# Two transformer blocks in one kernel: the output projections' last slabs tile by tile, GpSimd's norm factors in another order, and a weight ring that starts at another buffer

## The reference, cut to what matters

```python
# block 1
h = rms_norm(x, mix_pre_norm);  proj = h @ w_in          # 1024 x 2472, then conv, delta rule, attention
mixed = concatenate([o_gdn, o_mla]) @ w_out
x = x + rms_norm(mixed, mix_post_norm)
h = rms_norm(x, ffn_pre_norm)
f = square(relu(h @ w_up)) @ w_down
x = x + rms_norm(f, ffn_post_norm)
# block 2
mod = c @ w_ada + b_ada;  sh1, sc1, gt1, sh2, sc2, gt2 = split(mod)
h = modulate(rms_norm(x, g_pre_mix), sh1, sc1);  proj = h @ w_in_2
mix_out = (sigmoid(ga) * y_conv + sigmoid(gb) * y_attn) @ w_out_2
x = x + gt1 * rms_norm(mix_out, g_post_mix)
h2 = modulate(rms_norm(x, g_pre_mlp), sh2, sc2)
x = x + gt2 * rms_norm(square(relu(h2 @ w_mlp_in)) @ w_mlp_out, g_post_mlp)
```

## Time and profile before

| | |
|---|---|
| median of 3 runs | 3013.69 us (3012.06 to 3013.9) |
| profiled execution | 3016.73 us, span 3014.9 us |
| TensorE busy | 2878.8 us, 95% of the span |
| VectorE, GpSimd, ScalarE busy | 1600.4, 1022.5, 738.2 us |
| TensorE's mean granted clock | 0.983 of 2.4 GHz |

### The profile page before, as it was taken

The page is one execution under the profiler, slowest core; times in us unless marked ns, Lnnn a source line. Parts: engine busy times, 40 slices in busy tenths (PEclk is TensorE's granted clock), DMA queues, the critical chain, the costliest instruction groups (busy, mean ns, idle before and its releaser), DMA issues.

```text
span 3014.9 us, 42598 instructions
## 1 busy us (share of the span) xinstructions
PE 2878.8 (95%) x16394; PEld 2323.0 (77%) x16394; DVE 1600.4 (53%) x1957; ACT 738.2 (24%) x1485; POOL 1022.5 (34%) x706
## 2 busy tenths in 40 slices
PE   7999998979999999999899999989998999999998
PEld 6887567868788888888688886657877888888886
DVE  3455544662777777777832004773246445445546
ACT  3223654323301111111410004562124101110111
POOL 3321001438433333433433321212376332323332
PEclk9999999989999999999999999999999999999999
DMA  3210000023222223222311110001132111111111
GB/s 125 56 28 16 10 1 23 3 86 104 70 84 85 84 82 90 77 83 84 105 49 49 55 29 28 22 1 56 56 133 64 42 54 43 56 42 45 52 49 63
DMA packets 213439, 172.18 MB, mean 57 GB/s; under 512 B 15543, under 2 KB 188878, under 8 KB 213326
## 3 DMA queue, kind: packets, MB, share of 16 engines
q1 hardware_dynamic: 160670, 135.47, 14.6%
q10 hardware_dynamic: 52656, 35.13, 3.9%
HBM read 162.19 MB, written 8.39 MB: 57 GB/s over the span
## 4 chain that ended last, share of the span: by engine, by line
PE 86%; DVE 6%; ACT 3%; POOL 3%; issue 2%; DMA 1%; SPq 0%; ACTq 0%; POOLq 0%; DVEq 0%
PE ps L910 13%; PE ps L912 13%; PE ps L911 13%; PE ps L1338 8%; PE ps L1339 7%; PE ps L1340 7%; PE ps L1130 2%; PE ps L1036 2%; PE ps L929 1%; PE ps L931 1%; PE ps L930 1%; PE ps L1058 1%; PE ps L1534 1%; PE ps L1276 1%; PE ps L1277 1%
## 5 line engine op out<-in xcount | busy, mean ns | idle before, releaser
L295 POOL TENSOR_SCALAR slab_hi<-raw 128x1024 fp32r<-128x1024 f32 (+1 forms) x236 | 268.0, 1136 | 1513.8 <-PE ps L912 576.8
L910 PE MATMUL ps<-act_hi,slab_hi 128*128 128x512 f32 x1472 | 577.0, 392 | 9.0 <-POOL slab_lo L298 7.2
L298 POOL TENSOR_TENSOR slab_lo<-raw,slab_hi 128x1024 fp32r<-128x1024 f32 (+1 forms) x236 | 578.7, 2452 | 19.7
L912 PE MATMUL ps<-act_hi,slab_lo 128*128 128x512 f32 x1472 | 574.6, 390 | 0.0
L911 PE MATMUL ps<-act_lo,slab_hi 128*128 128x512 f32 x1472 | 574.3, 390 | 0.0
L2530 DVE TENSOR_TENSOR acc<-ps,acc 128x512 f32<-128x512 f32 x512 | 339.0, 687 | 197.4 <-PE ps L1340 197.1
L1338 PE MATMUL ps<-slab_hi,hid_hi 128*128 128x512 f32 x1024 | 403.5, 394 | 1.4 <-DVE acc L2530 1.4
L1339 PE MATMUL ps<-slab_hi,hid_lo 128*128 128x512 f32 x1024 | 399.3, 390 | 0.0
L1340 PE MATMUL ps<-slab_lo,hid_hi 128*128 128x512 f32 x1024 | 399.2, 390 | 0.0
L910 PEld LDWEIGHTS ps<-act_hi,slab_hi 128*128 128x128 f32 x1472 | 277.6, 189 | 66.7 <-POOL slab_lo L298 7.5
L1924 ACT ACTIVATE relu<-ps 128x512 f32<-128x512 f32 x128 | 77.1, 602 | 1025.6 <-PE ps L912 1013.7
(11 more groups left out here) (315 smaller groups left out, 4190.0 us busy)
## 6 DMA issues: line engine op xcount, KB each, us to landing
raw<-in_w_in SPq DMA_DIRECT2D x56, 512.0 KB, 3.8
w_ada<-in_w_ada ACTq DMA_DIRECT2D x48, 512.0 KB, 4.1
raw<-in_w_out SPq DMA_DIRECT2D x32, 512.0 KB, 3.6
raw<-in_w_up SPq DMA_DIRECT2D x32, 512.0 KB, 4.0
raw<-in_w_down SPq DMA_DIRECT2D x32, 512.0 KB, 3.5
raw<-in_w_mlp_in SPq DMA_DIRECT2D x32, 512.0 KB, 4.0
raw<-in_w_mlp_out SPq DMA_DIRECT2D x32, 512.0 KB, 3.5
x_tok<-in_x SPq DMA_DIRECT2D x8, 512.0 KB, 6.1
```

The source lines that it names most:

```text
L295: pool.tensor_scalar(self.hi[s][:, 0:width], self.raw[r][:, 0:width], 1.0, 0.0, ALU.mult, ALU.add)\
L298: pool.tensor_tensor(self.lo[s][:, 0:width], self.raw[r][:, 0:width], self.hi[s][:, 0:width].bitcast(F32), ALU.subtract).then_inc(self.spl ...
L910: pe.matmul(o, hi[:, w], a_hi[:, k, cols], start=(k == 0), stop=False)
L912: mm = pe.matmul(o, lo[:, w], a_hi[:, k, cols], start=False, stop=(k == nk - 1))
```

## The change

It has four parts. R2 starts at the buffer that R1 frees first (2, then 0, 1), and its two start waits are gone; four small buffers change places with it. In the output projections the last three slabs are done tile by tile, all of them behind `ready(15)`; the turns of EARLY follow tile 0 and tile 2 in place of slabs 13 and 14. GpSimd does split 12 ahead of the EARLY post factors and places pre factors between the splits of 14 and 15 and behind 15; the LATE factors come one by one, with the FFN's slab 1 among them and slabs 2 and 3 behind them. ScalarE and VectorE follow with single tiles. At the end of the first FFN R5's slab 0 is split behind factor ffn_post 6, slab 1 behind n3 5, instead of both behind ffn_post 7.

```diff
-        R2 = Ring(sem, GDN_PANELS, raws[:3], slab_hi[:3], slab_lo[:3], R1)
+        turned_on = (2, 0, 1)
+        R2 = Ring(sem, GDN_PANELS, [raws[r] for r in turned_on], [slab_hi[r] for r in turned_on],
+                  [slab_lo[r] for r in turned_on], R1, (*turned_on, 3))
...
-            R2.start(sp)
...
-            R2.start_split(pool)
...
+        LATE_NORMS = ((0, 4), (0, 5), (1, 4), (0, 6), (1, 5), (0, 7), (1, 6), (1, 7))
...
-                for m in range(first, 12):
+                for m in range(first, 13):
                     ring.split(pool, 0, m // ring.nraw, m)
                 norm_rstd(post, EARLY)
-                norm_rstd(pre, EARLY)
-                for m in range(12, 16):
+                for m, ts in ((13, ()), (14, (0, 1)), (15, (2, 3))):
                     ring.split(pool, 0, m // ring.nraw, m)
+                    norm_rstd(pre, ts)
                 ffn_splits(following, 0, range(1))
-                for j in range(2):
-                    ffn_splits(following, 0, range(1 + j, 2 + j))
-                norm_rstd(post, LATE)
-                norm_rstd(pre, LATE)
-                ffn_splits(following, 0, range(3, 4))
+                for n, t in LATE_NORMS:
+                    norm_rstd((post, pre)[n], [t])
+                    if (n, t) == (0, NT - 2):
+                        ffn_splits(following, 0, range(1, 2))
+                ffn_splits(following, 0, range(2, 4))
...
-                if (tag, t) == ("ffn_post", NT - 1):
-                    for j in range(2):
-                        R5.split(pool, 0, 0, j)
+                if (tag, t) == ("ffn_post", NT - 2):
+                    R5.split(pool, 0, 0, 0)
+                elif (tag, t) == ("n3", 5):
+                    R5.split(pool, 0, 0, 1)
...
-                for m in range(16):
+                for m in range(13):
...
-                    if m in (13, 14):
+                ring.ready(pe, 0, 15)
+                for t in range(4):
+                    for m in range(13, 16):
+                        mm = out_tile(ring, m, t, a_hi, a_lo)
...
+                    if t == 0:
                         pe.wait_ge(sem("mixed_done"), 16 * run + 12)
-                        turn(pre, acc, 0, scaled(pre, 0), ks=range(4 * (m - 13), 4 * (m - 13) + 4))
+                    if t in (0, 2):
+                        turn(pre, acc, 0, scaled(pre, 0), ks=range(2 * t, 2 * t + 4))
...
-                    if first:
-                        turn_done(pre, 0)
-                    up(i, 0)
+                    up(i, 0, as_split(pre, 0) if first else None)
...
+                late(0)
+                norm_full(pre, 0, act_hi, scale, bias, ks=range(4))
+                late(1)
+                late_square(4)
+                late(2)
+                norm_scale(pre, 4)
+                norm_full(pre, 0, act_hi, scale, bias, ks=range(4, KD))
+                late_square(5)
+                late(3)
+                norm_scale(pre, 5)
+                for t in (6, 7):
+                    late_square(t)
+                    norm_scale(pre, t)
                 norm_full(pre, 1, act_hi, scale, bias)
...
+                post_norm(post, row, EARLY, ready)
+                post_norm(post, row, (4,), ready)
+                norm_split(pre, 0, act_hi, act_lo, gain, ks=range(4))
+                post_norm(post, row, (5,), ready)
+                norm_split(pre, 0, act_hi, act_lo, gain, ks=range(4, KD))
+                post_norm(post, row, (6, 7), ready)
+                norm_split(pre, 1, act_hi, act_lo, gain)
```

More of the change, by code:

```diff
@@ L250, with __init__ @@
     SLOTS = 4
-    def __init__(self, sem, total, raws, his, los, after=None):
+    def __init__(self, sem, total, raws, his, los, after=None, order=range(SLOTS)):
         self.raw, self.hi, self.lo = raws, his, los
         self.nraw, self.nslab, self.total = len(raws), len(his), total
-        self.raw_full = [sem(f"w_raw_full{r}") for r in range(self.SLOTS)]
+        self.raw_full = [sem(f"w_raw_full{r}") for r in order]
         self.carrier = sem("wait_carrier")
@@ L401, in two_blocks @@
         probs = [sb(f"probs{i}", kb, [P, SEQ]) for i, kb in enumerate((9, 13, 17, 25))]
[L402 to L405, removed]
+        probs_t = [sb(f"probs_t{i}", kb, [P, HALF]) for i, kb in enumerate((37, 39, 199.25, 201.25))]
+        wq_nope = sb("wq_nope", 41, [P, 2, P])
+        wq_rope = sb("wq_rope", 42, [P, 2, P])
+        wk = sb("wk_pair", 43, [P, P])
         w_kv = sb("w_kv_all", 45, [P, 1024])
-        sm_max, sm_neg, sm_sum, sm_rec = [sb(n, 40 + 0.0625 * x, [P, 2, NT])
+        sm_max, sm_neg, sm_sum, sm_rec = [sb(n, 44 + 0.0625 * x, [P, 2, NT])
                                           for x, n in enumerate(("sm_max", "sm_neg", "sm_sum", "sm_rec"))]
@@ L1895, in out_projection, with late @@
                     take(1, 0, t)
-                norm_full(pre, 0, act_hi, scale, bias)
-                for t in range(4):
+                def late(t):
                     take(1, 1, t)
@@ L2488, in _, with post_norms @@
             dve.wait_ge(sem("post_gain_in"), 16)
-            for h, tiles in enumerate((EARLY, LATE)):
-                post_norm("mix_post", mix_post_row, tiles, lambda t: dve.wait_ge(sem(f"x_in{t}"), 32))
-                norm_split("n2", h, act_hi, act_lo, ffn_pre_gain)
+            def post_norms(post, pre, row, ready, gain=None):
+                post_norm(post, row, EARLY, ready)
[5 more added lines that the diff above has]
+                norm_split(pre, 1, act_hi, act_lo, gain)
+            post_norms("mix_post", "n2", mix_post_row, lambda t: dve.wait_ge(sem(f"x_in{t}"), 32), ffn_pre_gain)
             def modulation(i, j):
@@ L2721, in _ @@
             dve.wait_ge(sem("gate_rows_done"), 2)
-            for h, tiles in enumerate((EARLY, LATE)):
-                post_norm("mix_post2", gate_rows[0], tiles, lambda t: dve.wait_ge(sem(f"x_in{t}"), 48))
-                norm_split("n4", h, act_hi, act_lo)
+            post_norms("mix_post2", "n4", gate_rows[0], lambda t: dve.wait_ge(sem(f"x_in{t}"), 48))
             ffn_sums(R11, 1, "ffn_post2", gate_rows[1])
```

20 lines of the change are left out of this document (14 added, 6 removed).

## The result

The changed kernel takes **3019.36 us** (median of 20 runs, 3015.64 to 3026.77), the kernel before 3013.99 us (20 runs, 3009.67 to 3017.6). The ratio is 1.002 with a 95% interval of 1.0014 to 1.0027, so the change costs 4.2 to 8.1 us; the medians differ by 5.4. The forecast was 3016.0 us, range 3004 to 3024. The profiled execution of the changed kernel took 3025.83 us (span 3024.0), near the top of its own runs, so the 9.1 us by which its span is longer than that of before overstates the change.

What follows compares the result with a forecast made beforehand. TensorE was taken as the bound, its chain ending last for 86% of the span. Terms 0 + 1.8 + 1.6 - 1.1 = +2.3 us on 3013.7 gave 3016.0 us, range 3004 to 3024.

Steps and rivals of the forecast that it cites:

- A: Whole kernel: the forecast itself, waits change place; 3016.0 us, own range 3008 to 3020, chance 0.46.
- B: Projections: split 15 done in time, ready(15) waits at most 1.5 us; about 3005 us, chance 0.25.
- C: Projections: late 4 us wait stays; 3022 to 3026 us, chance 0.29; decides if first projection's last scale is later than 774.
- The opening, 0 forecast: Opening: panel 0 starts near 111.9, TensorE then waits for conv_tanh until 142.6; net 0, bounds -3.3 and +0.5.
- So the 3.9 us move from L910 to L965. I take 0: Opening: the wait ahead of panel 0 reappears behind panel 1, for panel 0's conv_tanh; net 0.
- First projection, +1.8 forecast: First output projection: 4.5 us wait at ready(15), 1.6 for the clock, late wait 1.5 instead of 4.06; net +1.8 us.
- the 1.6 forecast: First output projection: 1.6 us lost to the lowered clock behind the wait at ready(15).
- The lower bound: First output projection: without any turns in splits 13 and 14 (3.1 of the 4.5 us) it gains 1.0.
- Second projection, +1.6 forecast: Second output projection: +4.5 and +1.6 at ready(15), early waits of 5.9 us go; net +1.6 us, bounds -6 and +5.
- 3.4 us of turns: Second projection's late transposes: splits of slabs 2 and 3 run beside VectorE's first pairs, 3.4 us more of turns.
- R5, -1.1 forecast: First FFN to second block: earlier split of slab 0, TensorE starts at about 1495.1; -1.1 us, bounds -4 and +1.
- ScalarE's copies hidden: First output projection: the four copies that mixed_done asks for end at 741.4, hidden in the slow first tiles.

Runs made afterwards that it cites:

- E1: Kernel before with the opening's part alone (buffer order 2, 0, 1, start waits gone, four small buffers moved): 3018.49 us, +4.5, ratio 1.0013.
- E11: Kernel before with opening's part plus a wait for conv_silu_done, R5's moved splits, and two-slab tile-by-tile projections: 3007.74 us, -6.3, ratio 0.9976.
- E3: Kernel before with R5's two splits moved ahead in the FFN's end, alone: 3010.69 us, -3.3, ratio 0.9986.
- E8: Kernel before with both projections' part, two slabs tile by tile instead of three, GpSimd's factors placed differently: 3013.21 us, -0.3, ratio 1.0.
- E2: Kernel before with the part on both output projections alone: 3019.14 us, +5.1, ratio 1.0018.
- E7: Kernel before with both projections' part, but GpSimd keeps its old order (eight early factors, then splits 12 to 15): 3022.9 us, +9.4, ratio 1.0038.
- E9: E2 with the one wait for split 15 taken apart into three in tile 0, one ahead of each slab's products: 3020.81 us, +6.8, ratio 1.0023.
- E6: Kernel before with ring order 2, 0, 1 and moved small buffers, but both start waits kept: 3012.77 us, -0.8, ratio 1.0001.
- E4: Changed kernel with VectorE's post-norm of the fourth tile cut to 8 of 1024 columns in both projections: 3016.49 us, ratio to before 1.0002.
- E12: Changed kernel with the second ring's fourth and fifth split behind conv_silu_done, and split 15's wait taken apart into three: 3015.95 us, +1.9, ratio 1.0008.
- E5: E1 with GpSimd's fourth and fifth split of the second ring held behind conv_silu_done: 3011.78 us, -1.8 against before, ratio 0.9993.

## Why the prediction was right, and where its terms were off

The forecast (A, waits change place) is what happened: +5.4 us against +2.3, no wait of a part vanished without another in its place. B is out, since both waits for slab 15 are 4.5 us. C's point of decision, a last scale behind 774, was not reached: the late turn starts at 773.33, in a trace that is 2.0 us late already at slab 4, and the late wait shrank to 1.33 and 1.98 us.

The mechanism is right; that the sum came out as near as it did is in part luck. Run alone, the parts measured +4.5, +5.1 and -3.3 us where 0, +3.4 and -1.1 were forecast: R5's part, 2.2 us better than its term, hides half of what the opening's term missed.

**The opening, 0 forecast, the mis-sized step.** All instants stand: start at 112.00 (111.9 forecast), splits over the gate chain and over the product, wait until 143.01 (142.6). The term that was mis-sized is the sum behind it, "So the 3.9 us move from L910 to L965. I take 0". The waits grew by 2.2 us (3.86 + 1.94 before, 0.89 + 7.12 now), and the clock gave back only 1.5: behind the two waits before, 1.6 and 3.3 us were lost to it, behind the one wait now 3.4. That is the 0.7 us of the table, 48.2 against 47.5. Besides, I read the baseline from one trace, and in three of the six with the old ring order the second wait is 0.3 to 0.5 us and the clock takes 1.7 behind it. Against the mean of the six the new opening is 1.8 us (changed kernel) and 2.0 (E1) longer up to panel 2.

Another 2 us or so are lost before the first projection (484.6 to 486.6 us, mean 486.2, in the eight with the new ring order, 484.1 in the mean of the six with the old), where no instruction was changed. It is mostly a count of clock falls between 200 and 330 us. Seven of the eight have two, between 231 and 239 and between 309 and 318, and E11 the second alone (484.6). Of the six, before and E3 have two (near 237 and 250), E8 two (235 and 313), E2, E7 and E9 none (482.4 to 482.7). The fall of 309 to 318 us stands, where it occurs, within 1.1 us behind a wait of 1.93 us that all fourteen traces have; why the clock falls there in one kernel and not in another was not found. Neither the early start (E6 has the fall without it) nor anything else was shown to be its cause. This stays open, and so does how much of E1's +4.5 it is.

**First projection, +1.8 forecast.** Up to the second half of the FFN's panels the term was right: from slab 4 to them it took 93.5 us in the changed kernel and 92.3 in E2, 90.7 to 92.4 in six kernels with the old projection (mean 91.3), so 1.0 to 2.2 more. The wait was 4.52 (4.5), no wait at slab 12, the late wait 1.33 (1.5). The clock cost more than the 1.6 forecast: tile 0 took 7.05 us in the changed kernel, 6.0 in E2, for 18 products that take 4.2 at full speed (a panel's 48 take 11.19). The lower bound took 3.1 of the 4.5 us for turns in splits 13 and 14 (which makes a gain of 1.3, not 1.0); E4, with the fourth tile cut, took off 1.85. What I missed comes behind it: VectorE's second set of sums for the modulation in the FFN's first step starts 5.2 us later than before (786.52 against 781.32), GpSimd's next splits only 4.7 later (787.34 against 782.67), so three of the four sums take turns with a split instead of two, and TensorE waits 3.53 us at 792.78 (3.30 in E2) where it waited 2.27 at 786.85 before. By the end of the FFN, projection 0 costs 2.1 (E2) to 4.6 us.

**Second projection, +1.6 forecast**, measured +2.4 and +2.6. The waits are where they were put: 4.52 at slab 15, none in the early turn, 1.72 (2.1 forecast) ahead of the panels, 2.08 + 2.58 in the late transposes, where 3.4 us of turns were computed. The late wait stayed at 1.98 us.

**R5, -1.1 forecast**, measured -1.7 in five traces and -1.9 in E12; E3's median says -3.3. The mechanism is the computed one: TensorE now waits for VectorE's fifth pair.

**What limits the three-slab form** I had only by half. The prediction names the wait for split 15 and calls ScalarE's copies hidden. They are, by 1.9 us; E9 shows that they are the next limit, and E4 that VectorE's fourth tile makes up 1.85 of the 4.5 us. So the form has two late chains, split 15 and the copies behind the last pre factors. The second comes from the pre factors' place behind split 15. The first doesn't: with all factors ahead of the splits (E7) the wait for slab 15 is 4.66 and 6.12 us. Taking away the first alone (E9) gained nothing. E8, with both changed, has neither wait, and a new one of 2.44 and 3.10 us in the early transposes.

On the cause of the stretched instructions: by the Trainium skill, "SBUF — State Buffer", section "SBUF: two separate sides", a GpSimd instruction that reads SBUF and a VectorE instruction with two SBUF inputs block one another, and whichever starts first holds the shared ports for its whole length. The traces agree: in the changed kernel the instruction of 124.72 ends at 127.00, just behind the subtraction that ends at 126.94, and in E5, where the splits are held back, the two stretched instructions return to 0.19 and 1.23 us.

## What to carry to other kernels

Before a step of one engine is moved earlier, lay its duration over the other engine's timeline: an instruction that the two can't run together is only worth moving into a gap, and one wait that holds it back (E5) may be worth more than the early start. Work of many slabs gathered behind one wait, or tile by tile, needs its last slab sooner; check not only that slab but every chain that now ends later, since taking the first limit away (E9) uncovered the second. Build the baseline of a stage from more than one trace, where stretches of lowered clock come and go by 1.6 us.

## What was not expected of the hardware

A wait costs more than its length, but what the clock adds isn't set by the length. In the opening, full speed for the 16 small products and the next panel is 1.84 + 11.19 us. Behind the 7.12 us wait they took 3.57 + 12.85 (changed kernel), 3.4 us more; behind 2.6 us 1.94 + 12.73 (E5), 1.65 more, but 3.3 more in E11; behind the 1.94 us of the kernel before 3.3 more, and behind the 0.31 to 0.48 us of E3, E8 and E9 still 1.7. So the loss comes in steps of some 1.7 us, and a wait of half a microsecond can cost as much clock as one of 2.6. The clock also falls in the midst of unbroken work: the panel near 235 us took 12.8 instead of 11.2 us, with no wait ahead of it, in ten of the fourteen traces. And a VectorE instruction of 32 elements a partition can take 2.28 us beside a split: for small instructions on a chain the turns are far more than their own time.
